# A mixture-of-experts kernel: token lists of the first 128 ranks made on the chip, DRAM lists for the rest

## The reference, cut to what matters

```python
gate = g_w * e_w
expert_id = g_idx * EXPERTS_PER_GROUP + e_idx
...
def expert_block(args):
    xb, e = args
    hid = jax.nn.silu(xb @ w_gate[e]) * (xb @ w_up[e])
    return hid @ w_down[e]
...
out = jax.ops.segment_sum(y_sorted * w_sorted[:, None], tok, num_segments=n_tok)
```

## Time and profile before

| | before |
|---|---|
| median of 3 runs | 2100.34 us (2096.74 to 2102.54) |
| span of the profiled execution | 2094.7 us |
| PE busy | 2023.5 us, 97% |
| DVE busy | 1567.1 us, 75% |
| ACT busy | 1362.9 us, 65% |
| POOL busy | 358.0 us, 17% |
| mean granted TensorE clock | 0.982 |

### The profile page before, as it was taken

The page is one execution under the profiler, slowest core; times in us unless marked ns, Lnnn a source line. Parts: engine busy times, 40 slices in busy tenths (PEclk is TensorE's granted clock), DMA queues, the critical chain, the costliest instruction groups (busy, mean ns, idle before and its releaser), DMA issues.

```text
span 2094.7 us, 32415 instructions
## 1 busy us (share of the span) xinstructions
PE 2023.5 (97%) x9566; PEld 1677.0 (80%) x9566; DVE 1567.1 (75%) x1878; ACT 1362.9 (65%) x1744; POOL 358.0 (17%) x439
## 2 busy tenths in 40 slices
PE   7999999999998999999999989998799999999996
PEld 6888778888877888888888868887688888888883
DVE  4334453336568999999999986867799999999995
ACT  3452244433447888888888874325588888888884
POOL 1000000000022222222232200001322222222220
PEclk9999999999999999999999989998799999999998
DMA  7232213332459999999999984233889999999996
GB/s 286 92 99 71 82 61 122 102 100 102 160 148 342 357 380 380 388 385 372 383 376 386 393 319 148 91 150 131 275 331 375 382 378 380 376 379 390 392 374 259
DMA packets 166952, 560.15 MB, mean 267 GB/s; under 512 B 31552, under 2 KB 32800, under 8 KB 164848
## 3 DMA queue, kind: packets, MB, share of 16 engines
q1 hardware_dynamic: 138960, 510.72, 64.7%
q0 software_dynamic: 25488, 39.57, 5.5%
q10 hardware_dynamic: 2448, 9.14, 1.3%
HBM read 541.94 MB, written 51.97 MB: 284 GB/s over the span
## 4 chain that ended last, share of the span: by engine, by line
PE 87%; DVE 5%; DMA 5%; ACT 1%; issue 1%; POOL 1%; SPq 0%; POOLq 0%; DVEq 0%; ACTq 0%
PE bank L619 27%; PE bank L621 26%; PE bank L620 26%; PE bank L850 3%; PE bank L699 1%; PE bank L888 1%; DVE big L1428 1%; DMA big<-in_w_up 1%; PE bank L688 1%; DVE big L1678 1%; DVE bank L1674 1%; DMA raw<-in_w_down 1%; DMA big<-normed,metas 1%; PE bank L738 1%; DMA big<-y_rows 1%
## 5 line engine op out<-in xcount | busy, mean ns | idle before, releaser
L619 PE MATMUL bank<-w_hi,a_hi 128*128 128x512 f32 x1944 | 773.1, 398 | 5.1 <-DVE a_lo L1420 2.8
L621 PE MATMUL bank<-w_hi,a_lo 128*128 128x512 f32 x1944 | 760.5, 391 | 0.0
L620 PE MATMUL bank<-w_lo,a_hi 128*128 128x512 f32 x1944 | 758.4, 390 | 0.0
L1420 DVE TENSOR_TENSOR w_lo<-raw,w_hi 128x1024 fp32r<-128x1024 f32 x372 | 454.2, 1225 | 353.4 <-ACT w_hi L1025 328.9
L1025 ACT ACTIVATE w_hi<-raw 128x1024 fp32r<-128x1024 f32 x372 | 392.8, 1060 | 458.2 <-PE bank L621 435.3
L1420 DVE TENSOR_TENSOR w_lo<-big,w_hi 128x1024 fp32r<-128x1024 f32 x530 | 620.1, 1219 | 29.3 <-ACT w_hi L1025 23.7
L1025 ACT ACTIVATE w_hi<-big 128x1024 fp32r<-128x1024 f32 x530 | 549.2, 1063 | 107.1 <-PE bank L621 106.9
L619 PEld LDWEIGHTS bank<-w_hi,a_hi 128*128 128x128 f32 x1944 | 367.1, 189 | 79.5 <-issue 4.2
L621 PEld LDWEIGHTS bank<-w_hi,a_lo 128*128 128x128 f32 x1944 | 366.0, 188 | 79.2
L620 PEld LDWEIGHTS bank<-w_lo,a_hi 128*128 128x128 f32 x1944 | 366.9, 189 | 72.6
L1420 DVE TENSOR_TENSOR a_lo<-bank,a_hi 128x512 fp32r<-128x512 f32 x227 | 147.7, 683 | 39.2 <-ACT a_hi L1025 39.2
(11 more groups left out here) (199 smaller groups left out, 1707.0 us busy)
## 6 DMA issues: line engine op xcount, KB each, us to landing
big<-in_w_gate SPq DMA_DIRECT2D x260, 512.0 KB, 5.3
big<-in_w_up SPq DMA_DIRECT2D x254, 512.0 KB, 5.7
raw<-in_w_down SPq DMA_DIRECT2D x244, 512.0 KB, 5.7
raw<-in_a_w_in SPq DMA_DIRECT2D x64, 512.0 KB, 3.9
raw<-in_a_w_out SPq DMA_DIRECT2D x32, 512.0 KB, 3.3
big<-y_rows SPq DMA_DIRECT2D x12, 1024.0 KB, 7.4
big<-in_w_down SPq DMA_DIRECT2D x16, 512.0 KB, 7.9
raw<-in_b_w_in SPq DMA_DIRECT2D x16, 512.0 KB, 5.0
```

The lines of the kernel that those rows point to most:

```text
L619: pe.matmul(dst, left_hi, right_hi, start=first, stop=False)
L620: pe.matmul(dst, left_hi, right_lo, start=False, stop=False)
L621: return pe.matmul(dst, left_lo, right_hi, start=False, stop=last)
L1420: return nc.vector.tensor_tensor(dst, src, f32(hi), ALU.subtract)
```

## The change

The entries of all 32 experts' first 128 ranks are made by 0/1 products and kept in a table `tab` in SBUF (128 slots x 47 items x 3 words). `ranked_slots` now writes float32 matrices of a token's rank in its expert (any expert; one matrix per tile and choice), `sent` multiplies the chosen experts' one-hot rows with token number and target row, and PE multiplies the two (`slot_ids_of`, 8 products of 128x64, and `slot_weights`, 8 products of 128x32, per half). `first_tokens` and the new DVE function `slot_weights` write the sums to `tab`. The matrix `chosen` lies in the same memory as `tab`.

The DRAM lists stay for ranks of 128 and more. All 16 writes remain, one per tile and choice, but their place is beyond the bound for ranks under 128 (`over_places`), and the writes leave such entries out. They are issued together, after gathers 0, 1 and 2 (`list_overflow`). `load_extra` then waits until they have landed, loads the entries of items 32 to 46 to `tab` in a loop of 15 DMAs, and waits for these. The loop of items has no loads of entries any more, and `n` is read after `load_extra`. PE waits for the finished table (`rt.tab`) ahead of `x_transposes(0)`, and SP's loads to `spatial` and to the first half of `vbias` wait for the products and the table.

```diff
-                def list_tokens(h):
-
-                    pool.wait_ge(rt.placed, HALVES * L + h + 1)
-                    pool.wait_ge(rt.weighted, HALVES * L + h + 1)
-                    for t in range(h * HT, (h + 1) * HT):
+                def list_overflow():
+
+                    pool.wait_ge(rt.placed, HALVES * L + HALVES)
+                    for t in range(TT):
                         for k in range(2):
                             pool.indirect_dma_start(
                                 out=lists[L][:, :],
                                 out_offset=bass.IndirectOffsetOnAxis(ap=place[:, t, k:k + 1], axis=0),
-                                in_=payload[:, t, k, :], in_offset=None).then_inc(rt.listed, 16)
+                                in_=payload[:, t, k, :], in_offset=None,
+                                bounds_check=E * LISTED - 1, oob_is_err=False).then_inc(rt.listed, 16)
+                def load_extra():
+
+                    pool.wait_ge(rt.listed, 16 * 2 * TT * (L + 1))
+                    pool.wait_ge(rt.table, L + 1)
+                    with pool.Fori(E, E + EXTRA - 1) as i:
+                        b = pool.value_load(table[0:1, 1, bass.ds(i, 1)], min_val=0, max_val=E * BPE - 1)
+                        pool.dma_start(tab[:, bass.ds(i, 1), :].rearrange("p i w -> p (i w)"),
+                                       lst[:, bass.ds(b, 1), 0:3].rearrange("p b w -> p (b w)")).then_inc(M.extra, 16)
+                    pool.wait_ge(M.extra, 16 * (EXTRA - 1))
...
-                list_tokens(0)
                 pool.wait_ge(rt.stored[0], 16 * (L + 1))
                 pool.wait_ge(rt.stored[1], 16 * HT * (L + 1))
-                pool.wait_ge(rt.first, FIRST * L + 1)
-                gather_rows(0, xg, M.gathered)
-                pool.wait_ge(rt.first, FIRST * L + 2)
-                gather_rows(1, xg1, rt.second)
-                list_tokens(1)
-                pool.wait_ge(rt.listed, 16 * 2 * TT * L + 16 * 2 * TT)
-                load_ahead(2, ahead_g, M.ahead_g)
-                load_ahead(0, ahead_s, M.ahead_s)
-                gather(2)
+                pool.wait_ge(rt.first, L + 1)
+                gather_rows(tab[:, 0, 0:1], xg, M.gathered)
+                gather_rows(tab[:, 1, 0:1], xg1, rt.second)
+                pool.wait_ge(M.x_full, 2)
+                nc.gpsimd.tensor_copy(meta_g[:, 0:3], item_meta(2)).then_inc(M.meta_g, 1)
+                gather_rows(tab[:, 2, 0:1], xg, M.gathered)
+                pool.wait_ge(rt.tab, 2 * L + 2)
                 scale_by(0)
+                list_overflow()
                 if L == 0:
                     pool.wait_ge(g.fold_stored, 16 * 4)
                 load_gain(2 * L + 2, A["norm_mix_g"][1] if L == 0 else A["final_norm_g"])
-                pool.wait_ge(rt.table, L + 1)
+                load_extra()
                 n = pool.value_load(table[0:1, 0, TABLE - 1:TABLE], min_val=E - 2, max_val=ITEMS_MAX - 2) + 2
-                load_ahead(3, ahead_g, M.ahead_g)
                 with pool.Fori(2, n - 1) as i:
                     gather(i + 1)
-                    load_ahead(i + 2, ahead_g, M.ahead_g)
                     scatter(i - 2)
...
+                pe.wait_ge(rt.tab, 2 * L + 2)
                 x_transposes(0)
...
+            def sent(L, h):
+
                 ts = slice(h * HT, (h + 1) * HT)
...
+                for f in range(2):
+                    last = tt(sent_ids[:, :, :, f, :], r_oh_k[:, :, ts, :],
+                              ids_of[:, f, :, ts].rearrange("p k (t o) -> p k t o", o=1).to_broadcast([P, 2, HT, E]), ALU.mult)
                 chained(L, last)
```

More of the change, by code:

```diff
@@ L1554, in places, with counts_and_slots, ranks @@
+                tt(sent_w, r_oh_k[:, :, ts, :],
+                   r_w[:, ts, :].rearrange("p t (k o) -> p k t o", o=1).to_broadcast([P, 2, HT, E]), ALU.mult).then_inc(rt.weighted, 1)
+            def counts_and_slots(L):
+                nc.vector.tensor_copy(base1, bank[7][:, 4 * E:5 * E]).then_inc(rt.slots, 1)
+                nc.vector.tensor_copy(slot_ids, bank[7][:, 256:256 + P]).then_inc(rt.slots, 1)
+                dve.wait_ge(rt.slots, 2 * L + 2)
+            def ranks(L, h):
                 ts = slice(h * HT, (h + 1) * HT)
@@ L1571, in list_places @@
-            def list_places(L, h):
-                ts = slice(h * HT, (h + 1) * HT)
-                for k in range(2):
-                    last = nc.vector.tensor_reduce(r_place[:, ts, k:k + 1], r_oh[k][:, ts, :], AX.X, ALU.add)
-                chained(L, last)
-                nc.vector.tensor_scalar(place[:, ts, :], r_place[:, ts, :], -1.0, None, ALU.add).then_inc(rt.placed, 1)
-            def slots_and_base(L):
-                tt(base1, bank[7][:, 4 * E:5 * E], cf[:, C_BASE:C_BASE + E], ALU.add).then_inc(rt.slots, 1)
-                for i in range(FIRST):
-                    nc.vector.tensor_scalar(slot_ids[:, i * BLK:(i + 1) * BLK], bank[7][:, 256:256 + P],
-                                            float(i * LISTED + 1), None, ALU.add).then_inc(rt.slots, 1)
-                dve.wait_ge(rt.slots, (1 + FIRST) * L + 1 + FIRST)
@@ new lines, in ranks @@
+                if h:
+                    chained(L, tt(r_pos[:, ts, :], before, base1.rearrange("p (o e) -> p o e", o=1).to_broadcast([P, HT, E]), ALU.add))
+                    before = r_pos[:, ts, :]
+                for k in range(2):
+                    last = tt(r_mine[:, k, :, :], r_oh[k][:, ts, :], before, ALU.mult)
+                chained(L, last)
+                for k in range(2):
+                    last = nc.vector.tensor_reduce(r_rank[:, ts, k:k + 1], r_mine[:, k, :, :], AX.X, ALU.add)
@@ L1742, in moe @@
                 mark_chosen(L, 1)
-                places(L, 1)
+                early_slots(L)
+                ranks(L, 1)
                 ranked_slots(L, 1)
-                for i in range(FIRST):
-                    first_tokens(L, i)
-                list_places(L, 1)
+                first_tokens(L)
                 weights(L, 1)
+                over_places(L, 1)
+                slot_weights(L)
                 unit(0, 1).then_inc(M.lo, 1)
```

157 lines of the change are left out of this document (85 added, 72 removed).

## The result

The changed kernel takes 2138.43 us (median of 4 runs, 2134.00 to 2140.56), the kernel before 2099.28 us beside it (4 runs): a ratio of 1.0192, with a 95% interval of 1.0179 to 1.0205. So it is slower by 34 to 39 us. Forecast were 21 us; the upper end of the range, 2139, is 38.7 us above the median on which it was made, and the first measurement is 39.1 above the kernel beside it. The sign was right, the size was not.

What follows compares the result with a forecast made beforehand. PE was taken as the bound, with POOL's chain ahead of item 3's gather deciding: +7.2 us second stage, +13.2 first, sum 20.4, on the median 2100.34 giving 2121 us, 1.0% slower; range 2099 to 2139.

Steps and rivals of the forecast that it cites:

- The stall at item 2 goes: PE's wait for item 2's gather vanishes: 9.7 us gained in the second stage with the clock, 0 in the first.
- the late down weights: First stage: ACT's 8.0 us wait for item 0's down weights would hold `down(0)`, so no gain at item 2 there.
- A new wait ahead of item 3: PE stands 11.7 us at item 3 in the second stage; first stage +10.7 us, each plus 2.5 for the clock.
- 16 writes: POOL's list writes ahead of item 3's gather, at 0.96 us and 0.30 between them: 20.2 us in the second stage.
- 15 loads: POOL's loop of loads ahead of item 3's gather, at the queue's 1.0 us a turn: 15 us.
- Rival B: Loop of loads and landings are dear: 1.5 us a turn, longer landings; half 2139 us, all 2158. Chance 0.19.
- Landings and steps between: On POOL's chain to item 3: last write lands in 6.2 us, last load 5.0, gather 5.0, plus wakes and copies.
- What comes ahead of gather 0: Added DVE and PE work before item 0: +2.7 us in the second stage, +2.3 in the first.
- at 0.15 us each: Price of a product ahead of item 0; the eight weight products cost 1.2 us and a semaphore.
- First stage, front: Float32 products and DVE work delay the first stage's transposes of item 0 by 2.3 us, from 628.05 to 630.4.
- Clock behind the waits: After the wait at item 3 PE runs at the low clock and loses 2.5 us more in each stage.
- A, the short chain: POOL's chain is short enough for no stall at item 3: 2094.6 us, partly 2095 to 2110. Chance 0.22, its corner 0.04.

Runs made afterwards that it cites:

- the repetition: The unaltered changed kernel measured again in a later run beside the kernel before: 2132.87 us against 2098.42, ratio 1.0169.
- The single load under traffic: The changed kernel with only one of the 15 low parts of the table loaded, the other 14 left out: 2105.75 us, ratio 1.0014.
- spread: The changed kernel with its writes and loads in pieces of up to four in rounds 2 to 9, loads written out: 2095.82 us, ratio 0.9976.

## Why the prediction was right or wrong

The mechanism held in the main, and three terms of the sum were too small: a turn of the loop of loads (1.0 us forecast, 1.54 measured), a list write (1.26 forecast, 1.47 and 1.68 measured in the second and the first stage) and a float32 product (0.15 forecast, 0.46 measured at the clock of 0.50). The landings were put too high in the second stage and hid part of this.

**The stall at item 2 goes: right.** No idle time is ahead of it in either stage. In the second the stretch from `gate_up(0)` to item 2 shrinks by 7.1 us, 7.2 were forecast (5.1 in the repetition, where other waits stand in it). In the first the stretch from item 0 to item 2 shrinks by 4.1, where I had given nothing: the late down weights that I feared did not hold PE. ACT waits 1.5 us for the unit (1.3 in the repetition) and not 8.0. It is not that item 0 came later: in the repetition item 2's transposes start at 656.77, earlier than before, and ACT starts on the unit at 656.65, before at 660.94. Why it lands earlier is open. The gain is soon spent, as PE then waits longer at item 3.

**A new wait ahead of item 3: right in kind, too small.** In the second stage I had 11.7 us and it is 13.96 (12.36 in the repetition); in the first the whole of what I had for it, with the clock, was 10.9, and it is 22.3 (19.8 + 2.4, rounded), or 18.2 less the 4.1 gained at item 2. The sum hides larger errors of both signs. Measured from the end of item 0's transposes to the rows of item 3, I had 57.6 us; it is 61.4 in the second stage (1507.70 to 1569.13) and 65.0 in the first (639.67 to 704.70). The parts, second stage:

- *16 writes:* 20.2 forecast, 23.6 measured (1511.18 to 1534.74), and 26.8 in the first stage. The failed step is "at 0.96 and 0.30 between them" for every one: a median was used as a mean. The maximum of 1967 ns stood in the same row, whose mean is 1091 ns, which would have given 22.3 us. The rest is the new writes' own: eight of the 32 take 1.8 us or more, and their mean is 1288 ns. That left-out entries don't make a write cheaper was right.
- *15 loads:* 15 forecast, 23.6 measured. The failed step is "In the rows it runs beside the gather, so I take the queue's 1.0". The queue's 1.0 is right, but 0.53 us more pass from its last register operation to the start of the load: 1.54 a turn, in both stages. In the rows of before a gather ran up to the start of the load (1510.97 to 1512.03, the load at 1512.04, the last register operation at 1511.5), and this time was hidden behind it. With loads in a row nothing hides it. Rival B had the number by luck: its 1.5 added the load's own 0.57, which in fact runs beside the register work. The second stage's 23.6 also hold one gap of 2.48 us ahead of the last load, of unknown cause; the first stage's loads take 22.1. The experiments with 8 loads and without the loop bear the price out.
- *Landings and steps between:* from the end of the writes to the first load it is 3.1 us (5.5 forecast), from the end of the loads to the gather 3.4 (7.7), to the gather's rows 4.3 (5.0), and to the first write 3.5 (4.2). That is 8 us less than forecast, beside 12 more for writes and loads. It does not hold for the first stage, whose parts are 2.9 to the first write, 26.8 for the writes, 6.5 to the first load, 22.1 for the loads, 3.4 and 3.3. Up to the first load PE runs in both stages; the DMA share in that gap is 0.96 in the first and 0.41 in the second. For the last load and the gather, PE and the weight loads stand, and medians of a loaded system were too long. The figure of the Trainium skill's page that I had weighed and set aside ("DMA: Bandwidth & Descriptors", section "Anatomy of one DMA — SWDGE (gpsimd) path": about 2.0 us plus bytes over 436 GB/s) is near for the last load, whose data are there at most 2.84 us after its start. The single load under traffic, 6.5 us, is far from it, as the rows of before were.

**What comes ahead of gather 0: the products were mis-sized.** The failed step is "at 0.15 us each". That row counts 128 records with 18.9 us in all, and a float32 product leaves two records; a product of that row is 0.30 us. At the clock of 0.50 that the second stage's front has, one costs 0.46 (3.67 for eight). So both the count of records and the clock were missed, and together they make a factor of three. DVE's timeline shows the waits that follow from it, where I had counted 0.5 us for the first (one product and a semaphore) and 1.2 less an overlap for the second:

```profile
1500.11 0.20 DVE L1621 SCALAR_TENSOR_TENSOR tab<-bank,vbias 128x32 int32<-128x32 f32 x1 [2.47 <-PE bank L796]
...
1505.47 0.20 DVE L1479 TENSOR_TENSOR tab<-bank,vbias 128x32 f32<-128x32 f32 x1 [3.37 <-PE bank L805]
```

The four low parts start at 1505.58, right behind the second. Counted from the chosen experts that is 13.6 us (from 1491.99), before it was 5.7 (1461.89 to 1467.59): 7.9 later, not 3. From the stage's start `gate_up(0)` comes 7.3 later against the 2.7 forecast. My bound for both stages, "8 us where none is", was nearly reached in this one alone.

**First stage, front: the size was a matter of the clock.** +2.3 forecast, +10.5 in the one execution and +2.5 in the other. In the latter the higher clock makes the products short (2.50, 1.92, 2.00 and 1.87 us). The forecast's agreement with it is not to its credit, as the price per product was wrong there too.

**Clock behind the waits: right.** 2.5 us each forecast, 2.4 and 2.0 measured (2.6 and 1.9 in the other execution).

**Rivals.** A, the short chain, did not come true. With the chain moved out of the way the time is 2095.82 us, and it had 2094.6; that the two are so close is partly luck, as A counted 2.7 us for the second stage's front, which costs 7.3. B came true by half, in the price of its loop of loads, not in its landings; its half price of 2139 is about what was measured, for reasons of which the products are one. That I gave the cheaper turn the better chance was the wrong reading.

By the repeated run, the miss of 16 us in the span is: 7.5 in the first stage, nearly all in the chain on POOL, 6.9 in the second (4.6 of it ahead of `gate_up(0)`, 2.3 behind it), and 1.7 between the stages, which I can't place. The first execution's further 8 us are clock.

## What to carry to other kernels

Before a chain of small DMAs on one queue is moved ahead of a loop, price one turn of it where nothing covers it: the trace of a kernel in which other work stands ahead of each transfer shows only the part that sticks out. Divide a row's total by the number of operations that the code issues, not by the records, and take a price from rows with the clock of the place to which it goes. Where single times in a row are twice the median, sum with the mean. And work that is only needed by a late item is better put behind the gathers of the first items than ahead of them: the same 16 writes and 15 loads a stage cost about 40 us in a row (change against spread, both stages together), and PE waits for no gather with them in fours.

## What the runs showed of the hardware that I had not expected

- A loop on POOL that reads a number, computes an address from it and issues a load costs 1.54 us a turn: 1.02 of register work, beside which the load before takes its 0.54, and then 0.53 up to the start of the load. Written out, with only the source address computed, it is 1.15 (0.65 and 0.50).
- An indirect write of which nearly all entries are left out costs POOL no less than a full one (1026 ns in the median and 1288 in the mean, before 959 and 1091), and the times are uneven: 0.98 us for most, up to 2.0 for others, with 0.30 between them. What tells them apart is open.
- A product of 128x128 by 128x64 in float32 takes 0.46 us at a granted clock of 0.50, 1.2 GHz (3.67 for eight, with two records each); eight of 128x64 in bfloat16 take 0.61 us together at the same clock.
- From the start of a 1.5 KB load to the copy that waits for it are 2.8 to 3.0 us where the DMA share in between is under 0.05 (12 stages, in seven executions), and 4.3 to 6.5 us where it is 0.31 to 1.02 (six stages, in four executions). These are the kernels in which the loads stand in a row.
- The clock at the front of the first stage falls to 0.50 between 604 and 608 us and comes up again at 613 us in one execution of the changed kernel and at 628 in the other, with PE busy all the while. It is worth 8 us here, more than many a change.
